# HGRN outputs drawn into its chain, the first output weights loaded a stage earlier, and attention values and probabilities multiplied as rounded parts and rests

## What is computed

```python
def softmax_attend(q, k, v):                       # global attention
    s = jnp.einsum('bkgqd,bksd->bkgqs', q, k) * HEAD_DIM ** -0.5
    return jnp.einsum('bkgqs,bksd->bkgqd', jax.nn.softmax(s, axis=-1), v)

def step(state, xs):                               # HGRN2, chunk by chunk, in both directions
    qd_i, kd_i, v_i, at_i, fl_i = xs
    o_i = jnp.einsum('bhcd,bhde->bhce', qd_i, state) + jnp.einsum('bhij,bhje->bhie', at_i, v_i)
    state = state * fl_i[..., None] + jnp.einsum('bhcd,bhce->bhde', kd_i, v_i)
    return state, o_i

o_l = jnp.concatenate([a_l, b_l, c_l, d_l], axis=-1) @ w_out
```

## Time and profile before

| | us |
|---|---|
| median of 3 runs | 4490.98 (4489.02 to 4492.21) |
| the profiled execution | 4490.53 |
| its span | 4488.6 |
| PE busy | 3876.8 (86%) |
| DVE busy | 2077.2 (46%) |
| ACT busy | 1337.2 (30%) |
| POOL busy | 1068.1 (24%) |

### The profile page before, as it was taken

The page is one execution under the profiler, slowest core; times in us unless marked ns, Lnnn a source line. Parts: engine busy times, 40 slices in busy tenths (PEclk is TensorE's granted clock), DMA queues, the critical chain, the costliest instruction groups (busy, mean ns, idle before and its releaser), DMA issues. The chain is left out here.

```text
span 4488.6 us, 80710 instructions
## 1 busy us (share of the span) xinstructions
PE 3876.8 (86%) x33188; PEld 3120.3 (70%) x33188; DVE 2077.2 (46%) x2848; ACT 1337.2 (30%) x1837; POOL 1068.1 (24%) x844
## 2 busy tenths in 40 slices
PE   6999559678887999999997999469679788999997
PEld 3888435456766888888885887345557677888886
DVE  3465755565557332232235243755555564332334
ACT  5121333233333312211225221333243334222223
POOL 1000510004521322332332000510015413243333
PEclk9999679799998999999998999679889899999998
DMA  5444130000012111101120334130010021111112
GB/s 191 162 159 160 54 116 1 18 30 12 5 56 89 47 35 36 37 33 42 37 80 19 127 121 146 48 113 1 18 39 5 32 85 66 47 46 48 47 47 94
DMA packets 72136, 285.77 MB, mean 64 GB/s; under 512 B 8000, under 2 KB 11328, under 8 KB 66880
## 3 DMA queue, kind: packets, MB, share of 16 engines
q1 hardware_dynamic: 55744, 201.53, 13.0%
q10 hardware_dynamic: 16128, 80.49, 4.9%
HBM read 226.67 MB, written 47.45 MB: 61 GB/s over the span
## 5 line engine op out<-in xcount | busy, mean ns | idle before, releaser
L3241 DVE SCALAR_TENSOR_TENSOR y<-ps,taps,y 128x1023 f32<-128x1023 f32 (+1 forms) x132 | 134.2, 1016 | 864.8 <-DVEq L3239 858.3
L496 PE MATMUL ps<-h_hi,wu_hi 128*128 128x512 f32 x1680 | 460.0, 371 | 9.6 <-PEq L3141 9.6
L496 PE MATMUL ps<-h_hi,wu_raw_rest 128*128 128x512 f32 x1680 | 459.3, 371 | 0.0
L496 PE MATMUL ps<-h_whole_rest,wu_hi 128*128 128x512 f32 x1680 | 459.0, 371 | 0.0
L3333 POOL TENSOR_TENSOR wu_raw_rest<-wu_raw,wu_hi 128x1024 fp32r<-128x1024 f32 x84 | 201.3, 2397 | 1030.9 <-POOLq L3332 1030.9
L496 PE MATMUL ps<-h_hi,w_hi 128*128 128x512 f32 (+1 forms) x1200 | 313.8, 366 | 34.5 <-PEq L492 34.5
L496 PEld LDWEIGHTS ps<-h_hi,wu_hi 128*128 128x128 f32 x1680 | 294.4, 188 | 66.0 <-issue 9.9
L496 PEld LDWEIGHTS ps<-h_hi,wu_raw_rest 128*128 128x128 f32 x1680 | 294.6, 188 | 56.4
L496 PEld LDWEIGHTS ps<-h_whole_rest,wu_hi 128*128 128x128 f32 x1680 | 294.1, 188 | 56.3
L496 PE MATMUL ps<-h_hi,w_raw_rest 128*128 128x512 f32 (+1 forms) x1200 | 312.4, 364 | 0.0
L496 PE MATMUL ps<-h_whole_rest,w_hi 128*128 128x512 f32 (+1 forms) x1200 | 312.1, 364 | 0.0
(11 more groups left out here) (402 smaller groups left out, 7718.9 us busy)
## 6 DMA issues: line engine op xcount, KB each, us to landing
wu_raw<-in_w_up_dram SPq DMA_DIRECT2D x88, 512.0 KB, 3.3
w_raw<-in_w_in_dram SPq DMA_DIRECT2D x54, 512.0 KB, 4.6
ada_w<-in_ada_rest_dram ACTq DMA_DIRECT2D x27, 1024.0 KB, 6.1
rows<-rows ACTq DMA_DIRECT2D x42, 640.0 KB, 4.7
wd_raw<-in_w_down_dram SPq DMA_DIRECT2D x40, 512.0 KB, 4.2
ada_w<-in_ada_rest_dram ACTq DMA_DIRECT2D x27, 512.0 KB, 4.8
h_whole<-rows SPq DMA_DIRECT2D x20, 640.0 KB, 7.3
wd_raw<-in_w_out_dram SPq DMA_DIRECT2D x16, 512.0 KB, 3.3
```

The source lines that it names most:

```text
L496: mm = pe.matmul(ps[:, lo:lo + width], w[a][:, t, :], rhs[b][:, t, lo:lo + width], start=(t == 0 and i == 0), stop=(t == n_k - 1 and i == 2))
L3241: dve.scalar_tensor_tensor(y[:, s, lo + 1:hi], ps[s][:, lo:hi - 1], k.taps[:, s, 0:1], y[:, s, lo + 1:hi], ALU.mult, ALU.add).then_inc(own ...
```

## The change

It has four parts.

- **HGRN.** The outputs of pair 0 stand in between levels 3, 4 and 5 of pair 1, on PE and on DVE. Half of pair 1's widest level is copied by DVE. The last additions go to the `turned` banks. The outputs of pair 1 are cut in two: what lies within chunks, and what comes from the states for each group and direction, ordered by when the states are there.
- **Output weights.** The first tile of w_out is loaded in GDN's gate stage into a place of its own. POOL rounds it, ACT rounds tiles 1 to 3 after its eight rounded inputs, and DVE makes the first rest after one rest of inputs, and the next two after all of them.
- **Attention.** Values (once in each phase) and probabilities are split: ACT writes the rounded exponential and then the whole one from the same bank, POOL makes the rest, and PE multiplies values by probabilities in three fp32r matmuls. The third, with the probabilities' rest, comes one step later, between `products` and `values`. DVE's `output` of the block before moves from step 0 to step 1, behind `rows`.
- **Memory.** `masks` and the rounded probabilities lie over the mixers' constants, which SP loads again in `gdn_rows_phase` as its last load. The values' rest lies over the values, so POOL fills their columns of ones again before window attention.

The diff, cut to its core:

```diff
+                sp.dma_start(k.mix[:, 0:N_MIX - N_BASE], k.mix_source).then_inc(mix_back.sem, 16)
                 sp.wait_ge(values_in.sem, values_in.at(32))
+                sp.wait_ge(mix_back.sem, mix_back.at(16))
...
+    k.out_first = k.nc.alloc_sbuf_tensor_at(f"out_first_{k.count}", [P, KD, P], F32, offset=OUT_FIRST_AT)
+
+    def first_out_tile(sp):
+        sp.dma_start(k.out_first[:, :, :], a["w_out"][layer, 0]).then_inc(k.out_ahead.sem, 16)
+
+    gate_phase(k, k.oT[:, 0:2, :], 0, T_Z, V_GNORM, T if with_ctx else SEQ, first_out_tile)
...
 
         events = ([("diag", 0, e) for e in range(len(widths))] + lv(0, 0) + lv(0, 1) + lv(0, 2)
                   + [("diag", 1, e) for e in range(len(widths))] + lv(0, 3) + lv(0, 4) + lv(0, 5) + lv(1, 0)
-                  + lv(1, 1) + adds(0, 0) + lv(1, 2) + adds(0, 1) + lv(1, 3) + lv(1, 4) + [("out", 0, g) for g in both]
-                  + lv(1, 5) + adds(1, 0) + adds(1, 1) + [("out", 1, g) for g in both])
...
         def place_of(*event):
             return pairs[index[event] % 3]
+
+        def addition(a, d, g, r, i):
+
+            if (a, d, g) == (1, 1, 1):
+                return turned[r][:, HD * (i - 5 * g):HD * (i - 5 * g) + HD]
+            at = 512 * r + HD * (i - 5 * g)
+            return place_of("add", a, d, g)[:, at:at + HD]
...
+                if a == 1 and x == PAIRS - 1:
+                    eng.wait_ge(wide_done.sem, wide_done.at(event[3] + 1))
...
+
+        def widest_block(a, g, r, x):
+            c0, w = groups[g]
+            src = place_of("lv", a, PAIRS - 1, g)[:, :].rearrange("q (p y) -> q p y", p=2)[:, :, 0:w * HD]\
+                .rearrange("q p (c m) -> q p c m", m=HD)
+            keys = slice(HD * r + 32 * x, HD * r + 32 * x + 32)
+            cols = slice(32 * (1 - x), 32 * (1 - x) + 32)
+            return attn[keys, a, :, c0:c0 + w, cols], src[keys, :, :, cols]
...
-                        for r in both:
+                        for r in both[:1] if a else both:
                             for x in both:
-                                keys = slice(HD * r + 32 * x, HD * r + 32 * x + 32)
-                                cols = slice(32 * (1 - x), 32 * (1 - x) + 32)
-                                ins = act.activation(attn[keys, a, :, c0:c0 + w, cols], src[keys, :, :, cols], ACT.Copy)
+                                into, src = widest_block(a, g, r, x)
+                                ins = act.activation(into, src, ACT.Copy)
                         ins.then_inc(act_merged.sem, 1)
...
                             dve.scalar_tensor_tensor(states[a][:, d, j + 1, :], states[a][:, d, j, :],
                                                      tots[a][d][PAIRS - 1][:, chunk:chunk + 1],
-                                                     place_of("add", a, d, g)[:, at:at + HD], ALU.mult, ALU.add)\
+                                                     addition(a, d, g, r, i), ALU.mult, ALU.add)\
                                 .then_inc(state_done[d].sem, 1)
 
...
+                def widest(g):
+                    wait_products(dve, 1, PAIRS - 1, g)
+                    wait_read(dve, "lv", 1, PAIRS - 2, g)
+                    for x in both:
+                        into, src = widest_block(1, g, 1, x)
+                        ins = dve.tensor_copy(into, src)
+                    ins.then_inc(wide_done.sem, 1)
...
+                output(0, 0)
                 merge(1, 4)
-                output(0)
+                output(0, 1)
                 for g in both:
+                    widest(g)
                     scale_queries(1, PAIRS - 1, g)
                 scan(1, 0)
                 scan(1, 1)
-                output(1)
+                for g in both:
+                    output(1, g)
                 dve.wait_ge(out_added.sem, out_added.at(4))
...
-                    place = take_place("add", a, d, g)
+                    if (a, d, g) != (1, 1, 1):
+                        take_place("add", a, d, g)
                     pe.wait_ge(turn_taken.sem, turn_taken.at(9 + 6 * a + 3 * d))
...
                         i, r = j // 2, order(d, j % 2)
...
+                def within_chunks(a, g):
...
-                    pe.wait_ge(queries_scaled.sem, queries_scaled.at(scaled_before(a, PAIRS, g)))
-                    for d in both:
-                        pe.wait_ge(state_done[d].sem, state_done[d].at(19 * a + 19))
...
                     mm.then_inc(chunk_part.sem, 1)
+
+                def from_states(a, g, d, last):
+                    c0, w = groups[g]
+                    place = place_of("out", a, g)
                     pe.wait_ge(chunk_part.sem, chunk_part.at(2 * a + g + 1))
+                    pe.wait_ge(queries_scaled.sem, queries_scaled.at(scaled_before(a, PAIRS, g)))
+                    newest = max(when(d, c, r) for c in range(c0, c0 + w) for r in both)
+                    pe.wait_ge(state_done[d].sem, state_done[d].at(19 * a + newest))
...
+                                at = 512 * r + HD * (c - c0)
+                                mm = pe.matmul(place[half[p], at:at + HD], states[a][half[p], d, when(d, c, r), :],
+                                               queries_of(a, d)[half[p], 2 * c + r, :],
+                                               start=False, stop=last, skip_group_check=True)
+                    if last:
+                        mm.then_inc(out_done.sem, 1)
...
+                output(0, 0)
                 level(1, 4)
-                for g in both:
-                    output(0, g)
+                output(0, 1)
...
-                    output(1, g)
+                    within_chunks(1, g)
+                from_states(1, 1, 1, False)
+                from_states(1, 0, 0, False)
+                from_states(1, 0, 1, True)
+                from_states(1, 1, 0, True)
...
+                    pool.memset(VO[:, :, :, HD:P], 1.0).then_inc(zero_done.sem, 1)
                     for g in range(2):
+                        pool.wait_ge(zero_done.sem, zero_done.at(g + 1))
                         zero_queries(g).then_inc(zero_done.sem, 1)
-                        pool.wait_ge(zero_done.sem, zero_done.at(g + 1))
+                    pool.wait_ge(zero_done.sem, zero_done.at(3))
...
+        masks = k.nc.alloc_sbuf_tensor_at(f"masks_{k.count}", [P, 3, P], F32R, offset=MIX_AT + 4 * 3 * 512)
+        VO, VO_lo = VO
+        VO_hi = k.sb(st, "VO_hi", [P, 2, NT, P], F32R)
+        prob_hi = k.nc.alloc_sbuf_tensor_at(f"prob_hi_{k.count}", [P, 3, 512], F32R, offset=MIX_AT)
...
         negm = k.sb(st, "negm", [P, 3, 4])
         share = k.sb(st, "share", [HD, 2, 512])
-        sinks = k.sb(st, "sinks", [P, 3, 512])
+        if window:
+            sinks = extra[:, 0:2, :].rearrange("p a n -> p (a n)")[:, 0:3 * 512].rearrange("p (a n) -> p a n", n=512)
...
-                        pe.wait_ge(prob_done.sem, prob_done.at(u - 1))
+                        pe.wait_ge(whole_done.sem, whole_done.at(u - 1))
...
+                    pe.wait_ge(vo_lo_done.sem, vo_lo_done.at(g + 1))
                     pe.wait_ge(prob_done.sem, prob_done.at(u + 1))
                     for e, (key, h, q, w, at, out, bands) in enumerate(blocks[n].units[i]):
-                        mm = pe.matmul(outs[n % 2][:, out:out + w], VO[:, g, key, :], prob[:, u % 3, at:at + w],
-                                       start=(i == 0 and e == 0), stop=(i == len(blocks[n].units) - 1),
-                                       skip_group_check=True)
+                        for v in (VO_hi, VO_lo):
+                            pe.matmul(outs[n % 2][:, out:out + w], v[:, g, key, :], prob_hi[:, u % 3, at:at + w],
+                                      start=(i == 0 and e == 0 and v is VO_hi), stop=False, skip_group_check=True)
+
+                def values_of_rest(n, i):
+                    g, u = blocks[n].g, first_unit[n] + i
+                    pe.wait_ge(rest_done.sem, rest_done.at(u + 1))
+                    for key, h, q, w, at, out, bands in blocks[n].units[i]:
+                        mm = pe.matmul(outs[n % 2][:, out:out + w], VO_hi[:, g, key, :], prob_lo[:, u % 3, at:at + w],
+                                       start=False, stop=(i == len(blocks[n].units) - 1), skip_group_check=True)
                     mm.then_inc(pv_done.sem, 1)
...
+                        if i:
+                            values_of_rest(n, i - 1)
+                        elif n:
+                            values_of_rest(n - 1, len(blocks[n - 1].units) - 1)
                         values(n, i)
...
+                values_of_rest(count - 1, len(blocks[count - 1].units) - 1)
...
+                    act.activation(prob_hi[:, u % 3, 0:w], turned[u % 2][:, 0:w], ACT.Exp, scale=scale)\
+                        .then_inc(prob_done.sem, 1)
                     act.activation(prob[:, u % 3, 0:w], turned[u % 2][:, 0:w], ACT.Exp, scale=scale)\
-                        .then_inc(prob_done.sem, 1)
+                        .then_inc(whole_done.sem, 1)
...
```

(39 more changed lines are left out.)

81 lines of the change are left out of this document (43 added, 38 removed).

## The result

The kernel after takes 4512.13 us in the median of 5 runs (4505.59 to 4515.39), the kernel before beside it 4489.02 (4484.48 to 4492.21): ratio 1.0049, 95% interval 1.0034 to 1.0064, so 0.5% slower. The forecast was 4508. The profiled execution after takes 4512.40 us with a span of 4510.6, 22.0 us longer than the span before, where the forecast's sum was +17.7.

What follows compares the result with a forecast made beforehand. PE, busy 3876.8 of 4488.6 us, was taken as the bound, with chains it waits for. Terms -9.7 + 25.8 + 24 - 13 - 9.4 = +17.7 on 4490.53 gave 4508.2, stated as 4508 us, range 4470 to 4530.

Steps and rivals of the forecast that it cites:

- Window attention: Both layers' window stages: DVE's output queued behind the rows makes PE wait 4.1 us a block; +49.8 us with the clock.
- the chain: Window block: DVE's rows, output and third reduction in turn lengthen the period to 15.1 us; +25.8 with the phase ends.
- the clock: Window attention: granted clock falls to 0.50 behind each of twelve new PE waits, 2.0 us a fall; +24 us.
- what I had put down without rows: Ends of the window phases, where outputs wait for rest passes behind ACT and POOL: +1.3 and +3.5 us.
- The clock rival: Window attention: the clock holds at 1.00 through the new waits; kernel at 4484.7 us, chance 0.22.
- The rival of the other side: Window attention: the block keeps its cycle, PE's wait under 0.5 us; kernel faster at 4448 us, chance 0.13.
- POOL beside DVE: Attention: forecast 0; the rival had POOL slow DVE's reductions and outputs, +65 us, kernel at 4573, chance 0.06.
- The last rival: HGRN or output projection start: another engine is late there, nothing gained; kernel at 4518 to 4522 us, chance 0.09.
- HGRN: HGRN's end, both layers: shorter ACT copies and outputs started beside the scan; -6.5 us a layer, -13, bounds -10 and -17.
- Full attention: Full attention, both layers: three fp32r passes shorten later blocks by 0.55 us, the rest returns to waits; -9.7 us.
- Output projection: Output projection's start, both layers: earlier first weight tile and rests brought forward; -9.4 us, bounds -6 and -10.
- Edits at nothing: Constants' reload in the GDN rows, POOL's columns of ones and the values' parts are hidden behind other work: 0 us.

Runs made afterwards that it cites:

- experiment 3: Kernel after, plus 14 unread PE products ahead of each fourth maximum of window attention, filling the wait: 4498.49 us, ratio 1.0019 to the kernel before.
- experiment 5: Kernel before with only the change's HGRN mixer: 4472.77 us, ratio 0.9968 to the kernel before.
- experiment 6: Kernel before with only the early first tile of output weights and its roundings: 4482.85 us, ratio 0.9984 to the kernel before.
- experiment 4: Kernel before with only DVE's output moved to step 1 behind the rows of maxima, no split: 4548.82 us, ratio 1.0125 to the kernel before.
- experiment 11: Kernel after with DVE's output back at step 0, run a second time: 4449.12 us, ratio 0.9925 to the kernel before.

## Why the prediction was right

The total came right, 4508 against 4512.13, with the signs of all four terms and the mechanism of the largest; but the terms were off by 2 to 7 us each. That the total is off by only 4 is in part luck: HGRN gained 6.6 us more than forecast, and the other three together came out 11.5 us dearer.

**Window attention** was forecast at +25.8 for the chain and +24 for the clock, and measured +55.6. The chain's period of 15.1 is 15.0 in experiment 3, and its links are found one by one, each within 0.4 us, in the timeline of after. The clock's 2.0 us a block is 2.2 in the same comparison, which is some 2 of the 6 us that were missing. The other 4 belong to what I had put down without rows, and no run traces them to one place; it is not behind the last block, since from the last reciprocal on the stages take 4.7 and 4.6 us in both kernels. The growth lies between the first reciprocal and the last (26.6 and 20.6 us) and ahead of the first (3.8 and 4.6).

PE reached the fourth maximum at 8.15 (910.85 less 4.04, from 898.66), where I had 8.3. So what this term took from rows held, and what it took without rows did not.

**The clock** rival (4485) is refuted by the stretches at 0.50 in each block, and by experiment 3. The rival of the other side (4448), that the move costs nothing, needed a wait under 0.5 us and is refuted by the 4.04; but with the output at step 0 the kernel does take 4449 to 4454. **POOL beside DVE:** DVE's reductions of full attention take the same 1276 ns in the mean beside POOL as without it:

```profile
L2689 DVE TENSOR_REDUCE negm<-scores 128x1 f32<-128x1280 f32 (+1 forms) x40 | 51.1, 1276 | 80.9 <-PE scores L2570 80.8
```

```profile
L2778 DVE TENSOR_REDUCE negm<-scores 128x1 f32<-128x1280 f32 (+1 forms) x40 | 51.0, 1276 | 76.9 <-PE scores L2628 76.8
```

That agrees with the Trainium skill, "GPSIMD Engine Reference", section "Key points", by which DVE's instructions with two SBUF inputs or in a 2-port perf mode contend with POOL. This reduction has one input, and that in PSUM.

The last rival, that HGRN or the start of the output projection moves nothing, is refuted by experiments 5 and 6, whose intervals leave out 0.

**HGRN** was forecast at -13, measured -19.6, outside its own bounds of -10 to -17; it is the term most off. Two steps of it failed. I kept PE's work for the outputs at the 9.1 us that it took before, of which 5.56 ran at the granted clock of 0.50. Begun beside the scan, it is preceded by 0.49 us of idle time and not 3.54, has the low level only in its first 3 us and takes 7.6 (571.16 to 578.8) in layer 0:

```profile
571.00:574.00 3.00, 2.75 (x86) 2.56 (x88) 3.00 (x17) 0.00 (x0) 0.00 (x0) 0.50 0.00 0
...
577.00:578.80 1.80, 1.79 (x62) 1.65 (x58) 0.82 (x1) 0.00 (x0) 0.00 (x0) 1.00 0.00 0
```

In layer 1 the granted clock was 1.00 from 2915 on, and the stage ended 3.4 us behind the scan, not 9.1. And I put down for layer 1 what I had read in layer 0, where the scan's end moved by 3.0 us, and in layer 1 by 5.6. The change need not be different in the two layers: in the one profile of before that I had, layer 0's scan ends 118.2 us behind the stage's start, in experiments 4 and 6, with the same HGRN code, at 120.7 and 121.0. So layer 0's 3.0 is 3.0 to 5.9, and a term read from one profile has that uncertainty in it.

**Full attention** was -9.7, measured -6.5. The period shrank by 0.48 us (20.66 to 20.18), where the forecast had 0.55. Four later blocks of layer 0, before and then after:

```profile
681.16:763.59 82.43, 78.42 (x289) 48.42 (x289) 42.60 (x28) 26.25 (x44) 0.00 (x0) 1.00 0.00 1
```

```profile
672.33:752.78 80.45, 73.06 (x330) 55.48 (x329) 42.61 (x28) 45.81 (x85) 50.72 (x40) 1.00 0.00 1
```

PE's busy time shrank by 1.34 us a block, where I had 1.7, and the wait ahead of the third maximum took 0.64 of it, as forecast in kind. The rest of the error is in the ends of the phases: behind the sixth reciprocal layer 1 even loses 0.9 us (29.5 before, 30.4 after).

**Output projection** was -9.4; PE's matmuls of that projection run 5.0 and 4.8 us earlier in their stage, as forecast (4.7 each), and of layer 0's 5.0 us 2.4 are gone by the end of the stage, in steps along the ConvFFN, where the change does nothing. It may be no effect of the change at all: the eleven profiles with these weights have 1148.6 to 1153.9 us for layer 0's stage.

**Edits at nothing** held: the GDN rows stage takes 29.5 and 26.8 us after 29.1 and 28.5 before, and attention's rows, where POOL fills the ones, 20.7 in both.

## What to carry to other kernels

Moving an operation one step later on an in-order queue moves it behind everything that was issued in between, and here that was an operation which itself waited for two engines: 2.2 us a block, and as much again for the clock, for a line that computes the same. Before such a move, write the engine's queue out with start times from the trace and look for the first buffer that is released late. A wait of TensorE has two prices, its length and what the clock does behind it; keep the two apart by filling the wait with work that nothing reads. And once a chain on one engine holds a loop, shorten that chain's segment between release points first: taking 0.68 us out of it was worth 20 us on the medians, the whole split only 11.

## What the runs showed of the hardware that was not expected

- The same wait does not always have the same price. In the kernel with the output at step 0, a wait of 1.54 us in layer 1 was followed by 3.3 us at 0.50, in a block that took 14.06 us, while its neighbours with waits of 1.3 to 1.6 us kept 1.00 and took 12.4 to 12.6. The same kernel's second profile (experiment 11) has one such block in each layer, 14.04 and 14.07 us long:

```profile
3205.87 0.45 PE L2626 MATMUL scores<-KA,QA 128*128 128x256 f32 x1 [1.54 <-DVE negm L2778]
```

```profile
3206.10:3209.40 3.30, 3.30 (x14) 3.30 (x14) 1.25 (x2) 0.80 (x2) 0.38 (x1) 0.50 0.00 0
```

- Two kernels with the long wait have the same period though not the same work: the kernel after and the kernel before with the output at step 1 both take some 17.1 us a block, though the second has its values in fp32. In each of its turns the second has 3.41 us at 0.50 and 13.65 at 1.00 (experiment 4), the kernel after 6.83 and 10.24. Why the sum comes out the same was not tried.
